# Retention pipelined by head, and band attention with projections and output slabs between its heads

## The chip, the cores and the metric

The kernel runs on one core of one Trainium2 chip. The metric is the device time of one execution in microseconds (us). Engines: TensorE (matrix products), ScalarE (activations, copies), VectorE (elementwise), SyncE (issues the DMAs); GpSimd does next to nothing here.

## What is computed

Two blocks follow each other on 256 tokens of width 1024, all in float32. The first has two layers: layer 0 is a retention mixer and a dense SwiGLU, layer 1 a band attention and a mixture of 8 experts; each ends with a per-layer embedding. The second block (two layers of a hybrid mixer and an MLP) is not touched. What the change touches is this, cut from the reference:

```python
def retention_mixer(xn, positions, w_in, gn_gain, w_o):       # 4 heads, qk 256, v 512
    q, k, v, g = split(xn @ w_in)                             # widths 1024, 1024, 2048, 2048
    q, k = rotary(q), rotary(k) * 256 ** -0.5
    o = chunkwise_retention(q, k, v)                          # decay-weighted (q k^T) v, by head
    o = rmsnorm(o, gn_gain)                                   # over each head's 512
    return (silu(g) * o) @ w_o                                # 2048 -> 1024

def band_attention_mixer(xn, kp, vp, w_q, rel_table, w_o):    # 16 heads of 64
    s = q_c @ k_band^T + bias;  a = softmax(s);  o = a @ v_band
    return o @ w_o
```

At 256 tokens the band covers every earlier chunk.

## The kernel before

Tokens lie in two tiles of 128 (TT = 2), the width in eight chunks of 128 (KD = 8). Each engine runs its own stream of instructions in the order in which its function writes them, and waits on semaphores; nothing reorders them.

**Weights** come as slabs of 1 MB (128 x 2048 float32), in the order that `weight_stream` lists, into a ring of five slots (RING). A projection of 256 columns is one "tall" slab, one of 512 columns two "wide" slabs, and two row chunks of an output matrix one "rows" slab. Every product of two float32 matrices is made of three products of rounded parts (`split_products`, L211: high x high, high x low, low x high), so each slab is split first: ScalarE writes its rounded high part (`scalar_split`, L689) into one of three buffers (HIGHS), and VectorE subtracts it in place to leave the low part (`vector_lows`, L702). Both run two slabs ahead of the one in use (AHEAD), and the high part of slab n waits until slab n-3 has been read. Activations are split in the same way (`vector_norm` L645, `vector_split` L710 and L712) and announced on `parted`. Small products of attention (scores, values, transposes) are plain float32.

**Results** go to PSUM banks: two rings of two banks, `a` (drained by ScalarE) and `v` (drained by VectorE), and four banks that sum an output product.

**Retention** (`tensor_retention` and its namesakes on ScalarE and VectorE): after the norm, eight tall projections of q and k with the rotary on VectorE, four wide ones of v, the scores of the four heads, four wide ones of the gate g. Before the first rotary VectorE makes the table of sines (`vector_constants`). Then, for each head and token tile, values on TensorE (plain float32, 12 products of 512 columns), squares and a root on ScalarE (L997, L583), the gating on VectorE (L1039); after all heads (semaphore `gated`) 32 transposes (L968), gains (L1048) and a split per token tile; then the output product r.out, eight slabs.

**Band attention** (`tensor_band` and its namesakes): four tall projections of k, two wide ones of v, four tall ones of q, then the 16 heads in `tensor_attention` as a software pipeline: in each turn the scores of one head (two products), the three transposes of the probabilities of another (L1207), and the values of a third (two products). VectorE adds the bias and takes the maximum (L1284), ScalarE the exponentials (L1242), VectorE divides (L1300), ScalarE copies the transposed probabilities (L1268) and the head's result (L1275). After all heads VectorE splits the result, and the output product a.out reads its four slabs.

## Time and profile before

| | us |
|---|---|
| median of three runs | 2751.07 (2742.73 to 2752.49) |
| the profiled execution | 2758.43 |
| its span | 2756.60 |
| TensorE busy in the span | 2576.8 (93%) |
| VectorE, ScalarE busy | 1884.1 (68%), 1461.9 (53%) |

TensorE holds 83% of the chain that ended last, VectorE 11%, ScalarE 4%. The page's line of the granted TensorE clock, in 40 slices of 68.9 us, is 9 tenths or more in all slices but the ninth and tenth (6 and 7) and two at 8. The clock has two levels, 2.4 GHz (granted 1.0) and 1.2 GHz (0.5). A busy TensorE is not one that runs at its peak: its records get longer when the clock is lower. Retention lies between about 20 and 240 us of the span, band attention between 486 and 654.

### The profile page before, as it was taken

To read this page: it belongs to the slowest core of one execution; us is meant where nothing else is said; L and a number is where in the kernel's file an instruction comes from. 1 tells how busy PE (TensorE), PEld (TensorE's weight loads), DVE (VectorE), ACT (ScalarE), POOL (GpSimd) and SP (SyncE) were. 2 spreads that over 40 slices of the span, in tenths; PEclk is the share of its full clock that TensorE was granted. 3 is DMA by queue.
4 is the path that set the end of the run, shared out by engine and by line. 5 is a ranking of instruction groups with operands and counts; after the bars stand their busy time and mean duration, and the time that the engine had idled before them with its cause. 6 is when DMAs were issued, how large, how long until landed. Compare 5 with 4: busy or idle time off the path is not lost.

```text
span 2756.6 us, 32701 instructions
## 1 busy us (share of the span) xinstructions
PE 2576.8 (93%) x13559; PEld 2172.2 (79%) x13559; DVE 1884.1 (68%) x1960; ACT 1461.9 (53%) x1347; POOL 0.2 (0%) x4
## 2 busy tenths in 40 slices
PE   7989999896999999999999989799989999998999
PEld 7858897865788888888888777588758988876898
DVE  7454545545788888888888787557675556767554
ACT  3434334443666766767676666455544335555442
POOL 0000000000000000000000000000000000000000
PEclk9999999967999999999999999899989999998999
DMA  7534764415899999989899977255224554522453
GB/s 225 177 107 157 208 191 160 138 61 198 302 352 343 352 342 323 368 327 370 322 370 325 359 262 269 67 157 174 77 92 155 197 170 151 171 86 88 157 187 134
DMA packets 301812, 597.59 MB, mean 217 GB/s; under 512 B 13552, under 2 KB 105952, under 8 KB 301664
## 3 DMA queue, kind: packets, MB, share of 16 engines
q1 hardware_dynamic: 301664, 595.50, 62.7%
q8 instruction: 108, 1.77, 0.3%
q14 instruction: 40, 0.33, 0.0%
HBM read 594.41 MB, written 1.05 MB: 216 GB/s over the span
## 4 chain that ended last, share of the span: by engine, by line
PE 83%; DVE 11%; ACT 4%; issue 2%; DMA 1%; SPq 0%; DVEq 0%; ACTq 0%
PE ps L211 81%; DVE ring_rounded L702 2%; ACT high_rounded L689 1%; DVE arena_rounded L1884 1%; PE ps L1632 1%; PE ps L1207 1%; DMA ring<-in_w_down_dense 1%; DVE arena L2369 0%; DVE h L852 0%; DVE ring_rounded L1884 0%; DVE xT L639 0%; DVE xT_rounded L645 0%; DVE arena L2499 0%; DVE arena_rounded L712 0%; ACT high_rounded L1687 0%
## 5 line engine op out<-in xcount | busy, mean ns | idle before, releaser
L211 PE MATMUL ps<-high_rounded,arena_rounded 128*128 128x512 f32 x2664 | 838.0, 396 | 24.5 <-DVE arena_rounded L712 12.4
L702 DVE TENSOR_TENSOR ring_rounded<-ring,high_rounded 128x2048 fp32r<-128x2048 f32 (+3 forms) x231 | 513.5, 2231 | 328.3 <-ACT high_rounded L689 327.3
L689 ACT ACTIVATE high_rounded<-ring 128x2048 fp32r<-128x2048 f32 (+3 forms) x231 | 430.2, 1864 | 401.0 <-PE ps L211 386.6
L211 PEld LDWEIGHTS ps<-high_rounded,arena_rounded 128*128 128x128 f32 x2664 | 500.9, 191 | 130.5 <-DVE arena_rounded L712 14.3
L211 PE MATMUL ps<-ring_rounded,arena_rounded 128*128 128x512 f32 x1000 | 396.3, 396 | 0.0
L211 PE MATMUL ps<-xT_high_rounded,high_rounded 128*128 128x256 f32 x1280 | 365.8, 286 | 25.2 <-DVE xT_rounded L645 11.2
L211 PE MATMUL ps<-xT_high_rounded,ring_rounded 128*128 128x256 f32 x1280 | 364.0, 284 | 0.0
L211 PE MATMUL ps<-xT_rounded,high_rounded 128*128 128x256 f32 x1280 | 363.8, 284 | 0.0
L211 PE MATMUL ps<-arena_rounded 128*128 128x512 f32 x864 | 339.2, 393 | 0.0
L1884 DVE TENSOR_TENSOR arena_rounded<-arena,high_rounded 128x2048 fp32r<-128x2048 f32 x131 | 297.4, 2288 | 27.4 <-ACT high_rounded L1687 27.2
L1687 ACT ACTIVATE high_rounded<-arena 128x2048 fp32r<-128x2048 f32 x131 | 251.0, 1919 | 84.6 <-PE ps L211 83.2
L211 PEld LDWEIGHTS ps<-xT_high_rounded,high_rounded 128*128 128x128 f32 x1280 | 246.9, 193 | 30.6 <-DVE xT_rounded L645 12.0
L211 PE MATMUL ps<-high_rounded,xT_high_rounded 128*128 128x512 f32 (+2 forms) x640 | 250.5, 391 | 7.7 <-ACT arena L1144 3.1
L211 PEld LDWEIGHTS ps<-xT_rounded,high_rounded 128*128 128x128 f32 x1280 | 249.6, 195 | 0.0
L211 PEld LDWEIGHTS ps<-xT_high_rounded,ring_rounded 128*128 128x128 f32 x1280 | 246.4, 192 | 1.4
L211 PE MATMUL ps<-high_rounded,xT_rounded 128*128 128x512 f32 (+2 forms) x640 | 247.0, 386 | 0.0
L211 PE MATMUL ps<-ring_rounded,xT_high_rounded 128*128 128x512 f32 (+2 forms) x640 | 246.9, 386 | 0.0
L211 PEld LDWEIGHTS ps<-ring_rounded,arena_rounded 128*128 128x128 f32 x1000 | 191.0, 191 | 42.0
L211 PEld LDWEIGHTS ps<-arena_rounded 128*128 128x128 f32 x864 | 162.2, 188 | 35.7
L211 PE MATMUL ps<-arena 128*128 128x128 f32 (+7 forms) x776 | 168.4, 373 | 19.7 <-DVE arena_rounded L1896 5.0
L1884 DVE TENSOR_TENSOR ring_rounded<-ring,high_rounded 128x2048 fp32r<-128x2048 f32 x72 | 162.8, 2287 | 12.7 <-ACT high_rounded L1687 12.4
L211 PE MATMUL ps<-xT_high_rounded,arena_rounded 128*128 128x512 f32 x536 | 169.7, 398 | 1.1 <-DVE arena_rounded L1896 1.1
(282 smaller groups left out, 3084.3 us busy)
## 6 DMA issues: line engine op xcount, KB each, us to landing
arena<-in_w_down_moe SPq DMA_DIRECT2D x76, 1024.0 KB, 5.2
arena<-in_w_up_moe SPq DMA_DIRECT2D x72, 1024.0 KB, 5.8
arena<-in_w_gate_moe SPq DMA_DIRECT2D x68, 1024.0 KB, 5.4
ring<-in_w_in SPq DMA_DIRECT2D x50, 1024.0 KB, 5.1
ring<-in_w_gate_moe SPq DMA_DIRECT2D x44, 1024.0 KB, 5.4
ring<-in_w_up_moe SPq DMA_DIRECT2D x40, 1024.0 KB, 5.7
ring<-in_w_down_moe SPq DMA_DIRECT2D x36, 1024.0 KB, 5.3
ring<-in_w_up SPq DMA_DIRECT2D x32, 1024.0 KB, 5.4
```

The source lines that it names most:

```text
L211: return self.pe.matmul(out, lhsT, rhs, start=start, stop=stop, skip_group_check=True)
L689: act.activation(as_rounded(m, m.highs[n % HIGHS][:, 0:size]), m.slots[n % RING][:, 0:size], ACT.Copy).then_inc(m.rounded, 1)
L702: dve.tensor_tensor(as_rounded(m, slot), slot, as_rounded(m, m.highs[n % HIGHS][:, 0:size]), ALU.subtract).then_inc(m.slabs_split, 1)
L1207: ins = pe.transpose(bank[:, b * P:(b + 1) * P], p[:, b * P:(b + 1) * P], m.ident)
L1632: ins = pe.transpose(bank[:, c * P:(c + 1) * P], m.m_s[:, c * P:(c + 1) * P], m.ident)
L1687: act.activation(as_rounded(m, run.high(k)), run.slot(pos), ACT.Copy).then_inc(m.m_rounded, 1)
L1884: dve.tensor_tensor(as_rounded(m, slot), slot, as_rounded(m, run.high(k)), ALU.subtract).then_inc(m.m_split, 1)
```

## The change

Retention: the v projections now come first, on a first tile that needs only one token tile's parts (`tensor_wide_first`, there before); ScalarE and VectorE split the first two slabs among the parts of the norm (`opening`), and the table of sines stands behind the first v group. Of the four gate groups two come before the scores, one after them, and the last lies inside head 0. Values, norm, gating, transposes and split go head by head, and each head's two r.out slabs are multiplied while the next head is prepared.

Band attention: v's first half, k0 and q0 come first; the heads follow as turns, with one head's scores, the transposes and values of the one before, and one piece of other work between those: a half of a tall projection (`tensor_tall_half`: one bank, 256 columns), a tile of v's second half, or a half of an a.out slab (`tensor_rows_tile`). The splits of slabs that ran ahead of the heads are now inside the turns listed in BAND_SLABS. The pipeline is two heads deep where it was four. `tensor_head_values` and `tensor_head_turned` hold the products and transposes of one head that stood in `tensor_retention`; `vector_head_gated` and `vector_head_turned` the same for VectorE, with means and roots for both tiles at once.

```diff
win = w["w_in_a"][0]
     out = []
+    for h in range(HEADS_R):
+        out += wide("r.v", win, 2048 + h * DV_R)
     for h in range(2 * HEADS_R):
         out += tall("r.qk", win, h * DK_R)
-    for h in range(HEADS_R):
-        out += wide("r.v", win, 2048 + h * DV_R)
     for h in range(HEADS_R):
         out += wide("r.g", win, 4096 + h * DV_R)
     out += rows("r.out", w["w_out_a"][0], 0, 16)
     out += mlp_slabs("dense", (w["w_gate_dense"][0], w["w_up_dense"][0]), w["w_down_dense"][0],
                      FF_DENSE // STEP_FF)
     out += ple_slabs(w, 0)
-    for c in range(4):
-        out += tall("a.k", w["w_kv"], c * 256)
-    for g in range(2):
-        out += wide("a.v", w["w_kv"], D + g * 512)
-    for c in range(4):
-        out += tall("a.q", w["w_q_b"][0], c * 256)
+    keys = [tall("a.k", w["w_kv"], c * 256) for c in range(4)]
+    values = [wide("a.v", w["w_kv"], D + g * 512) for g in range(2)]
+    queries = [tall("a.q", w["w_q_b"][0], c * 256) for c in range(4)]
+    out += values[0] + keys[0] + queries[0] + keys[1] + queries[1] + keys[2] + queries[2]
+    out += values[1] + keys[3] + queries[3]
     out += rows("a.out", w["w_out_b"][0], 0, 8)
...
     for t in range(TT if casts else 0):
+        if opening:
+            scalar_split(act, L, m, 1 if t else -1)
         for half in range(2):
...
+        if opening and t == 0:
+            vector_lows(dve, L, m, 0)
...
+def tensor_tall_half(pe, L, m, w, f, x, ring):
+    if f == 0:
+        pe.wait_ge(m.slabs_split, L.read)
+    pe.wait_ge(ring.drained, L.room(ring))
+    bank = L.bank(ring)
+    for k in range(KD):
+        first, ins = L.split_products(bank[:, 0:S], [p[:, k, f * P:(f + 1) * P] for p in w],
+                                      [p[:, k, :] for p in x], k == 0, k == KD - 1)
+        L.give_back(first)
+    ins.then_inc(ring.full, L.up(ring.full))
+    if f:
+        L.done_with()
+    return L.emptied(ring)
...
+def tensor_rows_tile(pe, L, m, w, t, x, chunk, first, last):
+    n = w[0].shape[1]
+    for c in range(n):
+        for half in range(2):
+            end = last and c == n - 1
+            begin, ins = L.split_products(m.ps[:, 2 * t + half, :],
+                                          [p[:, chunk + c, t * P:(t + 1) * P] for p in x],
+                                          [p[:, c, half * 512:(half + 1) * 512] for p in w],
+                                          first and c == 0, end)
+            L.give_back(begin)
+            if end:
+                ins.then_inc(m.acc_full, L.up(m.acc_full))
+    if t:
+        L.done_with()
...
+def tensor_head_out(pe, L, m, h, half):
+    if half == 0:
+        pe.wait_ge(m.parted, L.next(m.parted))
+    if h == 0 and half == 0:
+        pe.wait_ge(m.acc_drained, L.sums_taken())
+    tensor_rows(pe, L, m, "r.out", parts(m, m.r_yT, m.r_yT_high), 4 * h + 2 * half, h == 0 and half == 0,
+                h == HEADS_R - 1 and half == 1)
 def tensor_retention(pe, L, m):
-    pe.wait_ge(m.parted, L.next(m.parted, 4))
+    x = parts(m, m.xT, m.xT_high)
+    tensor_wide_first(pe, L, m, "r.v", x, m.a)
+    for g in range(3):
+        tensor_wide(pe, L, m, "r.v", x, m.a)
     for h in range(2 * HEADS_R):
-        tensor_tall(pe, L, m, "r.qk", parts(m, m.xT, m.xT_high), m.v)
-    for g in range(4):
-        tensor_wide(pe, L, m, "r.v", parts(m, m.xT, m.xT_high), m.a)
+        tensor_tall(pe, L, m, "r.qk", x, m.v)
+    for g in range(2):
+        tensor_wide(pe, L, m, "r.g", x, m.a)
     for h in range(HEADS_R):
         if h == 0:
...
-    for g in range(4):
-        tensor_wide(pe, L, m, "r.g", parts(m, m.xT, m.xT_high), m.a)
+    tensor_wide(pe, L, m, "r.g", x, m.a)
     pe.wait_ge(m.v.drained, L.emptied(m.v))
     pe.wait_ge(m.a.drained, L.emptied(m.a))
+    tensor_head_values(pe, L, m, 0)
+    w = [L.slab("r.g"), L.slab("r.g")]
+    tensor_wide_tile(pe, L, m, w, 0, x, m.a)
+    tensor_head_turned(pe, L, m, 0)
+    tensor_wide_tile(pe, L, m, w, 1, x, m.a)
     for h in range(HEADS_R):
+        if h + 1 < HEADS_R:
+            tensor_head_values(pe, L, m, h + 1)
+        tensor_head_out(pe, L, m, h, 0)
+        if h + 1 < HEADS_R:
+            tensor_head_turned(pe, L, m, h + 1)
+        tensor_head_out(pe, L, m, h, 1)
...
+    head_sums(0)
+    scalar_split(act, L, m)
+    gate(3, 0)
+    scalar_split(act, L, m)
+    gate(3, 1)
+    for h in range(1, HEADS_R):
+        head_sums(h)
+        scalar_split(act, L, m, 2)
+    scalar_split(act, L, m, 2)
...
+    for g in range(4):
+        vector_lows(dve, L, m, 2)
+        if g == 0:
+            vector_constants(dve, L, m)
+    dve.wait_ge(m.sines, L.next(m.sines, 2))
...
-    dve.wait_ge(m.v.drained, L.at(m.v.drained))
-    dve.memset(m.small[:, 189:190], 0.0).then_inc(m.gated, L.up(m.gated, 8))
-    for t in range(TT):
-        for g in range(4):
-            dve.wait_ge(m.v.full, L.next(m.v.full))
-            bank = L.filled(m.v).rearrange("p (c n) -> p c n", c=4)
-            gain = m.gain[:, G_RET + 4 * g:G_RET + 4 * g + 4].unsqueeze(2).broadcast_to([P, 4, P])
-            dve.tensor_tensor(m.r_yT[:, 4 * g:4 * g + 4, t * P:(t + 1) * P], bank, gain, ALU.mult).then_inc(
-                m.v.drained, L.up(m.v.drained))
-        dve.wait_ge(m.v.drained, L.at(m.v.drained))
-        vector_split(dve, L, m, m.r_yT[:, :, t * P:(t + 1) * P], m.r_yT_high[:, :, t * P:(t + 1) * P])
-    vector_lows(dve, L, m, 8)
+        if h == HEADS_R - 1:
+            L.up(m.a.drained, 2)
+            dve.wait_ge(m.a.drained, L.at(m.a.drained))
+        vector_head_gated(dve, L, m, h)
+        vector_lows(dve, L, m)
+        vector_head_turned(dve, L, m, h)
+        vector_lows(dve, L, m)
+    vector_lows(dve, L, m, 2)
     vector_add_acc(dve, L, m)
...
+def tensor_band(pe, L, m):
+    x, x2 = parts(m, m.xT, m.xT_high), parts(m, m.xT2, m.xT2_high)
+    o = parts(m, m.a_o, m.a_o_high)
+    evicted = {}
+    held = {}
+    rows = lambda h: slice(DH * (h % 2), DH * (h % 2) + DH)
+    def project(name, c, f):
+        if f == 0:
+            held["w"] = L.slab("a.k" if name == "k" else "a.q")
+        evicted[name, c] = tensor_tall_half(pe, L, m, held["w"], f, x if name == "k" else x2, m.a)
+    def values(t):
+        if t == 0:
+            held["v"] = [L.slab("a.v"), L.slab("a.v")]
+        tensor_wide_tile(pe, L, m, held["v"], t, x, m.a)
+        evicted["v", 1] = L.emptied(m.a)
+    def product(c, t):
+        if t == 0:
+            held["o"] = L.slab("a.out")
+            pe.wait_ge(m.slabs_split, L.read)
+            pe.wait_ge(m.parted, L.next(m.parted))
+        tensor_rows_tile(pe, L, m, held["o"], t, o, 2 * c, c == 0, c == 3)
+    tensor_wide_first(pe, L, m, "a.v", x, m.a)
+    evicted["v", 0] = L.emptied(m.a)
+    for f in range(2):
+        project("k", 0, f)
+    pe.wait_ge(m.parted, L.next(m.parted, 4))
+    for f in range(2):
+        project("q", 0, f)
+    for turn in range(HEADS_A + 1):
+        if turn < HEADS_A:
+            if turn % 4 == 0:
+                pe.wait_ge(m.a.drained, max(evicted["k", turn // 4], evicted["q", turn // 4]))
+            tensor_scores(pe, L, m, m.a_q[rows(turn), turn // 2, :], m.a_k[rows(turn), turn // 2, :], m.v)
+        if turn:
+            pe.wait_ge(m.probs, L.next(m.probs))
+            tensor_turn_probs(pe, L, m, m.p_buf[(turn - 1) % 3])
+            turned = L.emptied(m.a)
+        if turn < 2:
+            project("kq"[turn], 1, 0)
+            project("kq"[turn], 1, 1)
+        elif turn < 6:
+            project("kq"[turn // 2 - 1], 2, turn % 2)
+        elif turn < 8:
+            values(turn % 2)
+        elif turn < 12:
+            project("kq"[turn // 2 - 4], 3, turn % 2)
+        elif turn == 12:
+            pe.wait_ge(m.acc_drained, L.sums_taken())
+            product(0, 0)
+            product(0, 1)
+        elif turn < 15:
+            product(1, (turn + 1) % 2)
+        elif turn == 15:
+            product(2, 0)
         h = turn - 1
-        if 0 <= h < heads:
-            vector_head_probs(dve, L, m, h, p[h % 3])
-def tensor_band(pe, L, m):
-    pe.wait_ge(m.parted, L.next(m.parted, 4))
-    for c in range(4):
-        tensor_tall(pe, L, m, "a.k", parts(m, m.xT, m.xT_high), m.a)
-    for g in range(2):
-        tensor_wide(pe, L, m, "a.v", parts(m, m.xT, m.xT_high), m.a)
-    pe.wait_ge(m.parted, L.next(m.parted, 4))
-    for c in range(4):
-        tensor_tall(pe, L, m, "a.q", parts(m, m.xT2, m.xT2_high), m.a)
-    pe.wait_ge(m.a.drained, L.emptied(m.a))
-    rows = lambda h: slice(DH * (h % 2), DH * (h % 2) + DH)
-    tensor_attention(pe, L, m, HEADS_A, lambda h: m.a_q[rows(h), h // 2, :], lambda h: m.a_k[rows(h), h // 2, :],
-                     lambda h, t: m.a_v[:, t, h * DH:(h + 1) * DH], m.p_buf, m.pT_buf)
-    pe.wait_ge(m.parted, L.next(m.parted, 2))
-    tensor_out(pe, L, m, "a.out", parts(m, m.a_o, m.a_o_high), 0, KD)
+        if h >= 0:
+            if h in (0, 8):
+                pe.wait_ge(m.a.drained, max(turned, evicted["v", h // 8]))
+            else:
+                pe.wait_ge(m.a.drained, turned)
+            tensor_values(pe, L, m, h, lambda t: m.a_v[:, t, h * DH:(h + 1) * DH], m.pT_buf[h % 2])
+    product(2, 1)
+    product(3, 0)
+    product(3, 1)
+    evict(m.a_v[:, 0, 0:512])
+    scalar_split(act, L, m)
+    evict(m.a_v[:, 1, 0:512])
+    scalar_split(act, L, m)
+    scalar_split(act, L, m)
+    for f in range(2):
+        evict(m.a_k[:, f, :])
+    scalar_split(act, L, m)
+    for f in range(2):
+        queries(0, f)
+    for turn in range(HEADS_A + 1):
+        h = turn - 1
+        if h >= 0:
+            scalar_turned_probs(act, L, m, m.pT_buf[h % 2])
+        if turn < HEADS_A:
+            scalar_head_exps(act, L, m, turn, m.s_buf[turn % 3], m.p_buf[turn % 3])
+        if turn == 0:
+            evict(m.a_k[:, 2, :])
+            evict(m.a_k[:, 3, :])
+        elif turn == 1:
+            queries(1, 0)
+            queries(1, 1)
+        elif turn in (2, 3):
+            evict(m.a_k[:, 4 + turn % 2, :])
+        elif turn in (4, 5):
+            queries(2, turn % 2)
+        elif turn in (6, 7):
+            evict(m.a_v[:, turn % 2, 512:1024])
+        elif turn in (8, 9):
+            evict(m.a_k[:, 6 + turn % 2, :])
+        elif turn in (10, 11):
+            queries(3, turn % 2)
+        if h >= 0:
+            scalar_head_out(act, L, m, h, m.a_o[:, h // 2, :])
+        if turn in BAND_SLABS:
+            scalar_split(act, L, m)
+    scalar_split(act, L, m)
+BAND_SLABS = (0, 1, 2, 4, 6, 7, 8, 10, 12, 13, 15)
+    def part(c):
+        at = slice(2 * c, 2 * c + 2)
+        dve.wait_ge(m.a.drained, L.at(m.a.drained))
         vector_split(dve, L, m, m.a_o[:, at, :], m.a_o_high[:, at, :])
-    vector_lows(dve, L, m, 4)
+    for turn in range(HEADS_A):
+        vector_head_logits(dve, L, m, turn, m.s_buf[turn % 3],
+                           lambda h, t: m.bias[:, h, TILE_KEYS[t]][:, ::-1], 1.0)
+        vector_head_probs(dve, L, m, turn, m.p_buf[turn % 3])
+        if turn in (5, 9, 13):
+            part(turn // 4 - 1)
+        if turn:
+            L.up(m.a.drained, 2)
+        if turn < 2:
+            L.up(m.a.drained, 2)
+        elif turn < 12:
+            L.up(m.a.drained)
+        if turn in BAND_SLABS:
+            vector_lows(dve, L, m)
+    L.up(m.a.drained, 2)
+    part(3)
+    vector_lows(dve, L, m)
```

How the order on the engines moves, at three places. ScalarE at the opening (`xn<-h` is the norm's sum of squares, `xT_high` the cast of normed parts, `high<-ring` a slab's high part), before:

```order
L601 ACTIVATE xn,small<-h 128x1024
L604 ACTIVATE small<-small 128x1
L614 ACTIVATE xT_high_rounded<-xT 128x4x128 x4
L689 ACTIVATE high_rounded<-ring 128x2048 x2
L913 ACT_TABLE_LOAD
```

and now:

```order
L599 ACTIVATE xn,small<-h 128x1024
L602 ACTIVATE small<-small 128x1
L692 ACTIVATE high_rounded<-ring 128x2048
L615 ACTIVATE xT_high_rounded<-xT 128x4x128 x2
L692 ACTIVATE high_rounded<-ring 128x2048
L615 ACTIVATE xT_high_rounded<-xT 128x4x128 x2
L692 ACTIVATE high_rounded<-ring 128x2048 x2
L1058 ACTIVATE arena<-ps 128x512 x2
L692 ACTIVATE high_rounded<-ring 128x2048 x2
L1058 ACTIVATE arena<-ps 128x512 x2
L950 ACT_TABLE_LOAD
```

One slab is rounded ahead of each token tile's casts, and the sines' table load has moved behind two v groups (L1058 is their copy out of PSUM). VectorE in the tail of retention, before (the last of eight gatings, the barrier, then gains and splits of whole token tiles):

```order
L588 TENSOR_SCALAR small<-small 128x1
L591 RECIPROCAL small<-small 128x1
L1039 SCALAR_TENSOR_TENSOR arena<-ps,small,arena 128x512
L1042 MEMSET small 128x1
L1048 TENSOR_TENSOR arena<-ps,gain 128x4x128 x4
L710 CAST arena_rounded<-arena 128x16x128
L712 TENSOR_TENSOR arena_rounded<-arena,arena_rounded 128x16x128
```

and now, for one head (`ring_rounded<-ring` is a slab's low part):

```order
L586 TENSOR_SCALAR small<-small 128x2
L589 RECIPROCAL small<-small 128x2
L1086 SCALAR_TENSOR_TENSOR arena<-ps,small,arena 128x512 x2
L705 TENSOR_TENSOR ring_rounded<-ring,high_rounded 128x2048
L1096 TENSOR_TENSOR arena<-ps,gain 128x4x128 x2
L713 CAST arena_rounded<-arena 128x1024
L715 TENSOR_TENSOR arena_rounded<-arena,arena_rounded 128x1024
L705 TENSOR_TENSOR ring_rounded<-ring,high_rounded 128x2048
```

The barrier is gone, and two slabs' low parts lie inside each head. ScalarE among the heads of band attention, before (copy of the transposed probabilities, two exponentials of the next head, again a copy, the head's result):

```order
L1268 ACTIVATE arena<-ps 128x384
L1242 ACTIVATE arena,small<-arena,small 128x128
L1242 ACTIVATE arena,small<-arena,small 128x256
L1268 ACTIVATE arena<-ps 128x384
L1275 ACTIVATE arena<-ps 64x256
```

and now, one turn with a slab:

```order
L1318 ACTIVATE arena,small<-arena,small 128x128
L1318 ACTIVATE arena,small<-arena,small 128x256
L1448 ACTIVATE arena<-ps 128x256
L1343 ACTIVATE arena<-ps 64x256
L692 ACTIVATE high_rounded<-ring 128x2048
L1336 ACTIVATE arena<-ps 128x384
```

Between the exponentials and the next copy of probabilities now stand a projection's copy (L1448), the head's result (L1343) and a slab's high part (L692).

## Rows read from the trace of the kernel before

**Rows 1.** Windows: stretch, length, busy TensorE, its loads, VectorE, ScalarE, GpSimd; clock, DMA.

```profile
19.70:26.50 6.80, 3.96 (x18) 3.99 (x19) 6.18 (x8) 3.50 (x3) 0.00 (x0) 0.50 1.08 366
165.40:193.40 28.00, 17.14 (x57) 8.27 (x57) 16.13 (x34) 10.09 (x26) 0.00 (x0) 0.95 0.11 38
190.40:197.30 6.90, 5.56 (x18) 4.75 (x19) 6.06 (x7) 0.00 (x0) 0.00 (x0) 0.51 0.00 0
...
497.10:500.90 3.80, 3.75 (x19) 3.75 (x20) 3.80 (x5) 1.59 (x1) 0.00 (x0) 0.56 0.00 0
...
567.70:626.90 59.20, 56.47 (x176) 31.65 (x176) 22.86 (x128) 28.98 (x96) 0.00 (x0) 0.57 0.05 19
572.70:623.90 51.20, 50.94 (x146) 28.51 (x146) 19.39 (x108) 24.13 (x82) 0.00 (x0) 0.50 0.00 1
...
631.20:654.00 22.80, 22.76 (x94) 18.73 (x95) 5.91 (x5) 4.56 (x6) 0.00 (x0) 0.94 0.42 139
...
1923.00:1960.00 37.00, 35.10 (x212) 29.98 (x211) 33.89 (x45) 17.04 (x15) 0.00 (x0) 1.00 0.34 114
```

**Rows 2.** Timeline of the opening: start, length, instruction, idle time before it.

```profile
13.04 0.63 ACT L614 ACTIVATE xT_high_rounded<-xT 128x512 fp32r<-128x512 f32 x1 [4.36 <-DVE xT L639]
14.63 1.47 DVE L645 TENSOR_TENSOR xT_rounded<-xT,xT_high_rounded 128x512 fp32r<-128x512 f32 x2
22.54 0.55 PE L211 MATMUL ps<-xT_high_rounded,high_rounded 128*128 128x256 f32 x1 [5.62 <-issue]
24.56 0.28 DVE L879 CAST arena<-arena 128x256 f32<-128x256 int32 x1
30.99 0.29 DVE L905 TENSOR_SCALAR arena<-arena 128x256 f32<-128x256 f32 x1
37.44 0.36 PE L211 MATMUL ps<-xT_high_rounded,high_rounded 128*128 128x256 f32 x1 [1.56 <-DVE arena L1014]
```

**Rows 3.** DMAs of slabs issued from 6 to 7 us, their landing.

```profile
L2761 SPq DMA_DIRECT2D ring<-in_w_in_a x3: 434/655/4834, 5.6 to 6.8; - x3
...
DMA to landing us min/median/max: 9.3/11.9/14.2
```

**Rows 4.** Timeline of TensorE in the tail of retention.

```profile
164.37 0.40 PE L211 MATMUL ps<-ring_rounded,xT_high_rounded 128*128 128x512 f32 x1
165.50 2.81 PE L211 MATMUL ps<-arena 128*128 128x512 f32 x6 [0.73 <-issue]
...
184.07 1.09 PE L968 MATMUL ps<-const,arena 128*128 128x128 f32 x8 [2.45 <-DVE small L1042]
...
193.36 1.20 PE L211 MATMUL ps<-high_rounded,arena_rounded 128*128 128x512 f32 x2
```

**Rows 5.** Timeline of band attention, by engine.

```profile
491.84 1.47 DVE L645 TENSOR_TENSOR xT_rounded<-xT,xT_high_rounded 128x512 fp32r<-128x512 f32 x2
...
561.76 1.90 ACT L689 ACTIVATE high_rounded<-ring 128x2048 fp32r<-128x2048 f32 x1
563.70 2.29 DVE L702 TENSOR_TENSOR ring_rounded<-ring,high_rounded 128x2048 fp32r<-128x2048 f32 x1 [3.47 <-ACT high_rounded L689]
569.45 0.92 PE L211 MATMUL ps<-arena 64*128 64x128 f32 x4 [0.84 <-DVE small L1284]
...
624.13 0.55 PE L1207 MATMUL ps<-const,arena 128*128 128x128 f32 x3
624.23 0.38 ACT L1275 ACTIVATE arena<-ps 64x256 f32<-64x256 f32 x1 [0.78 <-PE ps L211]
624.76 0.84 PE L211 MATMUL ps<-arena 128*64 128x256 f32 x4
```

**Rows 6.** Chain that ended last: start, length, engine, line.

```profile
497.15 69.86 PE ps L211 x480
...
568.75 0.29 DVE arena L1284
...
571.45 0.55 PE ps L1207 x3
```

176 lines of the change are left out of this document (71 added, 105 removed).

## The prediction

> **What bounds the kernel now.** I read the page's line of the granted clock first (the section on the profile tells it), to see where TensorE runs slowly, and found the one long dip in the band attention and just behind it. Then the table of windows [rows 1], to see in the stretches that the change touches whether TensorE waits, runs slowly, or neither; then the timelines and the chain there [rows 2 to 6]. Nearly everywhere TensorE is busy and ends the chain, so a change gains only what TensorE waits, or what it runs at 1.2 instead of 2.4 GHz. Both are to be found here. In the tail of retention, 165.4 to 193.4, TensorE is busy 17.14 of 28.00 us. Between 572.7 and 623.9, the heads of band attention, it is busy 50.94 of 51.20 us, but at a granted 0.50, the lower level: that is a loss the busy share hides. ScalarE and VectorE are busy 24.13 and 19.39 us there, so under half [rows 1].
>
> All sums are made against the profiled execution: span 2756.60, run 2758.43 us, so 1.83 us lie around it. That run is 7.4 us above the median 2751.07 of the three runs; I take the gain off the median.
>
> **Opening of retention.** The first product was r.qk and is now r.v with a wide first tile, which needs only the first token tile's parts and one slab at a time. Before, it started at 22.54, after VectorE's subtractions of both tiles and the first slab's low part, and waited another 1.56 us at 37.44, because VectorE made the sine table between two slabs [rows 2]. Now ScalarE rounds slab 0 ahead of its casts. Slab 0 is issued at 5.6 and lands 9.3 us later, at 14.9; the third, issued at 6.8, lands 14.2 later, at 21.0 [rows 3], so one comes every 3 us. So: high part 14.9 + 1.9 (a slab's high part, 561.76 in [rows 5]) = 16.8, cast 0.6 = 17.4, VectorE's two subtractions 1.5 = 18.9 [rows 2], low part 2.3 (563.70 in [rows 5]) = 21.2. TensorE starts 1.2 us earlier. But the clock is at the lower level until 26.5 in the window from 19.7 [rows 1], TensorE having stood idle after its transposes, so of 1.2 us only 0.6 is work done. The sine table now falls under the first r.v groups, whose tiles take 5.7 us each. The first tile, 2.6 us of it done at 26.5, ends at 29.5, the second at 35.2, the second group at 46.5. Slab 0 is read in the middle of the second tile, 32.4, so slab 3's high part ends at 34.3 and its low part at 36.6; the table, 24.6 to 31.3 before [rows 2], adds 6.7, and slab 4's low part 2.3: 45.6, and TensorE wants it at 46.5. The 1.56 us goes, with a cover of 0.9 us only. **Gain 0.6 + 1.6 = 2.2 us.** Bounds: 0.6 if that cover fails, 4.8 if the early start keeps the clock up (2.6 more).
>
> **Tail of retention.** From the end of r.g at 164.8 to the first r.out product at 193.4 are 28.6 us [rows 4]. TensorE's own work in it is 12 value products, three in 2.81, so 11.2 us, 32 transposes at eight in 1.09 to 1.25, some 4.7 us, and 0.7 us in which the last gate is evicted (it stays). 28.6 - 16.6 = 12.0 us are waits for norm chains, the barrier after all heads and VectorE's splits. The clock then sits at 0.51 from 190.4 to 197.3, with TensorE busy 5.56 of it [rows 1]: 2.8 us lost, 0.6 of them in the transposes counted already, 2.2 in the first out products. Now a group r.g and the 16 r.out half-products stand between the heads. Is the cover enough? Head 0, from the start of its values: second product ends 2.8, ScalarE squares it by 3.6, means, table load 1.28, root and reciprocal by 5.5, VectorE gates both tiles by 7.0; TensorE has a gate tile until 2.8 + 5.5 = 8.3. For later heads: values of h+1, then 5.4 us of r.out (two row slabs per head, 24 products each; eight slabs took 46 us with the slow start), then its transposes. Again about 1.3 us spare. The table is loaded twice more and ScalarE evicts the same eight tiles: all under these products. The two slabs per head need 4.2 us of ScalarE and VectorE each, against 15 us per head. **Gain 12.0 + 2.2 = 14.2 us.** Bounds: 9 if each of four heads comes 2.5 us later than reckoned (1.3 covered), 15.
>
> **Start of band attention.** The parts of the first token tile are ready at 493.3 [rows 5]; the first projection started at 497.15 [rows 6] since it waited for all four. The wide first tile starts on two: 3.85 us. The second tile's parts come at 497.1, its products at 498.9. The idle time ahead of 497.15 was followed by a lower clock, 0.56 over 497.1 to 500.9 [rows 1], so 3.3 us at half and 1.7 lost; without that gap I take it as gone. **Gain 5.5 us**, bounds 3.8 and 5.5.
>
> **Heads of band attention.** 16 heads took 59.2 us (567.7 to 626.9) [rows 1]. At the full clock one head's work is 0.92 (scores) + 0.50 (three transposes; the row's 0.55 overlaps its neighbour) + 0.84 (values) [rows 5], 2.26 us, 16 of them 36.2: 23.0 us less. Now the projections k1, q1, k2, q2, v1, k3, q3 and the first five half-slabs of the out product stand between. Does the clock hold? The nearest stretch in the trace is 1923 to 1960, where 2.8 us pieces of a projection alternate with 2 us of small plain-fp32 products and TensorE also waits a little (busy 35.10 of 37.00): granted 1.00 [rows 1]. So yes, in the forecast.
>
> The out product used to wait 4.3 us (626.9 to 631.2) for the split of all heads, and ran its first part slowly: 0.94 over 22.80 us [rows 1] is 1.4 us lost. Now only the last two chunks' split is late, and a 2.7 us half-slab lies over it. 5.7 us.
>
> Against that stands a **new wait**. The slabs' rounding, which had finished before the heads, now lies inside 11 of the turns on ScalarE and VectorE, in order with the softmax. Let V be the end of a head's values on TensorE in a turn with a slab. ScalarE copies the head out (0.38), rounds the slab, VectorE subtracts: from 561.76 to the end of the latter's 563.70 row are 4.2 us [rows 5]. Only then come the next head's maxima on VectorE, the exponentials and the division: 2.70 us from 568.75 to the transposes at 571.45 [rows 6]. With 0.1 us of hand-over the probabilities are ready at V + 7.4. TensorE gets to those transposes after a whole turn and the next scores. A half projection is half of 5.68 us (68.2 us for 12 slabs, the 69.86 of [rows 6] less 1.7), so a turn is 0.92 + 0.50 + 2.84 + 0.84 = 5.1 and it is there at V + 6.0: it waits 1.4 to 1.5. If the turn after has a whole projection (turns 1, 7) it is there at V + 8.7 and waits for nothing. If the turn after has a slab too, the ScalarE and VectorE loop sets the pace, about 7.0 us a turn, and 1.9 are waited. Slabs are in turns 0, 1, 2, 4, 6, 7, 8, 10, 12, 13 (15 has none left to round). The waits: after 1, 4, 7, 12 some 1.5 each, after 2, 8, 13 some 1.8, after 10 about 1.9 (the scores of head 12 wait for the last query's eviction behind the exponentials). Sum 13.3. The wait for the first query's eviction, 0.7, is as before. **Gain 23.0 + 5.7 - 13.3 = 15.4 us.** Bounds for the waits: 0 and 20.
>
> **Sum.** 2.2 + 14.2 + 5.5 + 15.4 = 37.3. Profiled 2758.4 - 37.3 = 2721; median 2751.1 - 37.3 = 2714 us. Behind the band nothing is reordered, and the experts' slabs start no later. The DMA queue fetches the same slabs in another order and holds them longer; among the heads its share was 0.05 [rows 1], so it has room.
>
> **Rivals.** B, *no new waits*: the rounding slips into gaps, the heads are bound by TensorE alone: 13.3 us more, 2701. Against it the in-order queues; for it that each wait is under 2 us, so small errors of mine cancel it.
>
> C, *the waits cost clock*: each of the eight waits comes with a stretch at the lower level as after 19.7 and 190.4, where 6.8 and 6.9 us ran at half [rows 1], 3.4 us a piece: 27 us for all, 2741; for half of them 2727. For it speaks that waits here are followed by such stretches; against it that those waits were 3.5 us and longer, and that 1923 to 1960 held through waits of 0.5 and 1.1.
>
> The Trainium skill's page TensorE: Matmul & The Clock Gate says, under A second HAM failure mode, that short pauses between groups of matmuls that cycle through PSUM banks make the clock swing; that is this rival, and speaks against the change.
>
> D, *slower than before*: the heads' small fp32 products alone hold the clock down, projections or not. The row 572.7 to 623.9 shows that TensorE need not be idle for it. Then everything from the first scores to the last values is at 1.2 GHz: 59 us of projections and out products double, the heads lose their 23 again, the 13.3 of waits are covered: 69 us on top, 2783. It decides from the point where 54% of that stretch is at half (37.3 of 69). The row of 1923 to 1960 speaks against it.
>
> On the same page, under What's actually happening, an idle TensorE is what brings the lower clock and activity what lifts it. This trace disagrees for the heads: 99% busy and 0.50. By the page alone the heads would have had the full clock already, the 23.0 us would not be there to gain, and the time would be 2737; the row decides.
>
> E, *retention's cover is too thin*: 5 to 8 us less, 2720.
>
> **Chances.** Forecast 0.55, B 0.15, C 0.18, D 0.04, E 0.08. The range takes in B with the opening's 2.6 more, 2697, and C for half of the waits together with E, 2736; the three runs before spread over 10 us, which is less. What 0.5% can tell is about the limit of measuring this kernel, 13.8 us. Only D is above 2765; a full C, or C with E, ends between 2737 and 2765. Faster 0.92, same 0.04, slower 0.04.
>
> **What would show it.** Opening: first product about 21.3, no wait of 1 us or more in the first 60 us. Tail: from the last gate tile of the third group to the last r.out product no wait over 1 us, clock 1.00. Band: first product as soon as two parts are there; heads at clock 0.95 or more; waits of 1.4 to 1.9 us on the division of the probabilities in turns 3, 4, 6, 9, 10, 14 and 15, on the scores in turn 12, none in 2 and 8, summing to some 13; no wait over 1 us ahead of the last out products. Wrong would be: a clock near 0.5 among the heads (D), waits absent (B), or waits in retention on the gating of a head (E).

## The result and the profile after

The changed kernel took 2706.03 us (median of 4 runs, 2699.85 to 2708.31) where the kernel before took 2751.78 beside it (4 runs, 2742.73 to 2754.20): ratio 0.9829, 95% interval 0.9808 to 0.9849. The gain is 45.7 us where 37.3 were forecast; 2706 lies inside the range 2697 to 2736. The same kernel was run five more times later: 2711.38 beside 2749.69, ratio 0.9853, interval 0.9834 to 0.9871. So the gain is some 38 to 46 us, and the forecast of 37.3 stands just below it. (Gains in us are differences of medians; a ratio is made of all the runs, so it can differ from theirs in the fourth digit.)

The page of the profiled execution after (span 2698.0 us, the shortest of all its runs), with its busy tenths in 40 slices and the granted clock of TensorE:

```profile
span 2698.0 us, 32714 instructions
PE 2526.2 (94%) x13559; PEld 2136.9 (79%) x13559; DVE 1883.0 (70%) x1959; ACT 1465.1 (54%) x1353; POOL 0.2 (0%) x4
...
PEclk9999999998999999999999999999989999998999
```

In the page of before the ninth and tenth digits of the clock were 6 and 7: the heads of band attention at half the clock, and the router behind them. The heads' part is gone; the 8 that is left there, in the slice from 607 to 674, holds the router's stretch. (Two more digits of 8 stand in both pages, and the page of before has a third.) TensorE runs the same 13559 products in 50.6 us less busy time (2576.8 before), which is most of the 58.6 by which the two spans differ. So most of the difference is the same products at a higher clock, and only the rest is idle time removed. A part of it lies behind the band, in code that the change doesn't touch; the table by stage below takes that out.

Windows of the changed stretches after (columns: stretch, its length, busy time and instructions of each engine, granted clock, share of the DMA engines, GB/s). They answer [rows 1]:

```profile
20.50:148.40 127.90, 127.75 (x752) 112.44 (x752) 80.24 (x81) 53.85 (x41) 0.00 (x0) 0.99 0.58 195
148.40:218.20 69.80, 68.76 (x297) 52.85 (x296) 43.46 (x44) 30.79 (x37) 0.00 (x0) 1.00 0.45 151
467.60:606.20 138.60, 126.67 (x750) 104.17 (x751) 66.90 (x164) 68.15 (x140) 0.00 (x0) 0.98 0.35 114
512.20:515.60 3.40, 3.40 (x17) 3.40 (x18) 1.62 (x1) 2.24 (x2) 0.00 (x0) 0.54 0.00 0
```

The first line is retention up to the third gate group: TensorE is never without work. The second is the pipelined heads with the last gate group and the out product: 1.04 us idle, clock 1.00, where the tail before held 10.86 us of idle time in 28.00 [rows 1, 4]. The third is all of band attention from the first projection: the clock is back at 0.98, but 11.9 us are idle, and 10.8 of them are the new waits that the prediction named. The fourth line is explained below.

Timeline of TensorE after (start, duration, engine, line, operation, tiles, shape, count, and in brackets the idle time ahead and what ended it): the first product of retention, then every place behind the first product of the band where TensorE waited, but for the 0.47 before the first scores. It answers [rows 2, 5]:

```profile
20.53 0.47 PE L211 MATMUL ps<-high_rounded,xT_high_rounded 128*128 128x512 f32 x1 [4.45 <-DVE ring_rounded L705]
...
512.18 0.67 PE L1298 MATMUL ps<-const,arena 128*128 128x128 f32 x3 [1.44 <-DVE arena L1368]
518.89 0.55 PE L1298 MATMUL ps<-const,arena 128*128 128x128 f32 x3 [0.16 <-DVE arena L1368]
530.39 0.55 PE L1298 MATMUL ps<-const,arena 128*128 128x128 f32 x3 [1.45 <-DVE arena L1368]
552.13 0.55 PE L1298 MATMUL ps<-const,arena 128*128 128x128 f32 x3 [1.44 <-DVE arena L1368]
558.84 0.55 PE L1298 MATMUL ps<-const,arena 128*128 128x128 f32 x3 [1.77 <-DVE arena L1368]
571.29 0.92 PE L211 MATMUL ps<-arena 64*128 64x128 f32 x4 [1.79 <-ACT arena L1448]
586.26 0.55 PE L1298 MATMUL ps<-const,arena 128*128 128x128 f32 x3 [1.55 <-DVE arena L1368]
592.43 0.55 PE L1298 MATMUL ps<-const,arena 128*128 128x128 f32 x3 [1.24 <-DVE arena L1368]
597.59 0.86 PE L211 MATMUL ps<-arena 128*64 128x256 f32 x4 [0.58 <-ACT arena L1336]
```

L1298 is the transposes of a head's probabilities, L1368 VectorE's division of them. These are turns 3, 4, 6, 9, 10, 14 and 15, and the scores of head 12: the eight places that the prediction named. The ninth row, 0.58 us before the values of the last head, is one that it did not name. The chain of waits through one of them (start, duration, what), which answers [rows 6]:

```profile
523.53 1.92 ACT high_rounded L692
525.46 0.02 issue
525.48 2.29 DVE ring_rounded L705
527.77 0.20 DVE arena L1352
...
528.36 0.18 DVE small L1357
528.54 0.02 issue
528.57 0.99 ACT arena L1318 x4
529.56 0.02 issue
529.58 0.18 DVE small L1364
529.76 0.02 issue
529.78 0.56 DVE arena L1368 x2
530.35 0.04 issue
530.39 0.55 PE ps L1298 x3
```

ScalarE rounds the slab (L692), VectorE subtracts (L705), and only then come the next head's maxima (L1352), the exponentials (L1318), the division (L1368) and TensorE. From the start of L692 it is 6.86 us to the transposes.

**Stage by stage.** One profile is one run, and the experiments below brought more profiles with the old or the new form of each stage. The table gives each stage from marks that all have: the last addition of retention's out product to the residual, the first product of the band, the start of the last pair of additions of its out product.

| stage | old form | new form | gain | forecast |
|---|---|---|---|---|
| to the last addition of retention | 240.4 (mean of 9, 238.6 to 241.9) | 219.4 (mean of 4, 218.9 to 220.3) | 21.0 | 2.2 + 14.2 |
| from there to the first band product | 254.2 (10, 252.1 to 257.0) | 251.3 (4, 248.8 to 252.7) | 2.9 | 3.85 |
| first band product to last additions | 157.8 (3, 156.9 to 159.6) | 138.7 (3, 138.6 to 138.9) | 19.1 | 17.1 |
| behind the band (the code is the same) | 2096.8 to 2102.6 | 2091.8, 2098.5, 2099.9, 2103.3 | none | 0 |

The forecast of the third row is 15.4 plus the 1.7 us of clock that the prediction counted with the start. The rows sum to 43.0 us, between the 45.7 and the 38.3 of the two comparisons. The profiled executions alone differ by 58.6 us: the profile of before is near the long end of its stretch behind the band (2102.6), the first one of after is the shortest of all (2091.8), on the same instructions. That is 10.8 us which the change did not make.

### The profile page after: what moved, and what is told of

It is laid out like the page before. It is cut to its first block, busy times and chain, and to the rows that moved or that the text cites. A ratio compares the mean times of both kernels' runs of the same rounds, so it can differ in the third digit from the quotient of the medians.

```text
span 2698.0 us, 32714 instructions
## 1 busy us (share of the span) xinstructions
PE 2526.2 (94%) x13559; PEld 2136.9 (79%) x13559; DVE 1883.0 (70%) x1959; ACT 1465.1 (54%) x1353; POOL 0.2 (0%) x4
## 4 chain that ended last, share of the span: by engine, by line
PE 81%; DVE 11%; ACT 4%; issue 2%; DMA 1%; SPq 0%; DVEq 0%; ACTq 0%
PE ps L211 80%; DVE ring_rounded L705 3%; ACT high_rounded L692 2%; DVE arena_rounded L2040 1%; PE ps L1788 1%; DMA ring<-in_w_down_dense 1%; DVE arena L2525 0%; DVE h L890 0%; DVE arena L2655 0%; DVE ring_rounded L2040 0%; ACT arena L1318 0%; DVE xT_rounded L646 0%; DVE xT L640 0%; DMA ring<-in_w_in_a 0%; PE ps L1298 0%
## 5 line engine op out<-in xcount | busy, mean ns | idle before, releaser
L705 DVE TENSOR_TENSOR ring_rounded<-ring,high_rounded 128x2048 fp32r<-128x2048 f32 (+3 forms) x231 | 513.2, 2230 | 289.9 <-ACT high_rounded L692 288.9
L692 ACT ACTIVATE high_rounded<-ring 128x2048 fp32r<-128x2048 f32 (+3 forms) x231 | 430.4, 1864 | 365.3 <-PE ps L211 339.0
L211 PEld LDWEIGHTS ps<-high_rounded,arena_rounded 128*128 128x128 f32 x2664 | 494.5, 188 | 125.2 <-DVE arena_rounded L715 9.0
L211 PE MATMUL ps<-xT_high_rounded,high_rounded 128*128 128x256 f32 x1280 | 362.2, 283 | 14.7 <-DVE xT_rounded L646 8.4
L211 PE MATMUL ps<-xT_rounded,arena_rounded 128*128 128x512 f32 x528 | 166.7, 397 | 0.0
```

Source lines behind the costliest of these rows:

```text
L211: return self.pe.matmul(out, lhsT, rhs, start=start, stop=stop, skip_group_check=True)
L692: act.activation(as_rounded(m, m.highs[n % HIGHS][:, 0:size]), m.slots[n % RING][:, 0:size], ACT.Copy).then_inc(m.rounded, 1)
L705: dve.tensor_tensor(as_rounded(m, slot), slot, as_rounded(m, m.highs[n % HIGHS][:, 0:size]), ALU.subtract).then_inc(m.slabs_split, 1)
```

## The experiments

All of them are compared with the kernel before, run on the same chip.

**1. Each half alone.** Are the two halves independent, and what is each worth? The first kernel has the change's retention and the old band (and the old order of its slabs), the second the old retention and the change's band:

```
first kernel:   retention (slab order, opening, tensor, scalar, vector) of the change; band of before
second kernel:  band (slab order, tensor, scalar, vector) of the change; retention of before
```

> The change's retention (opening and head pipeline) with the band attention of before. Theory T (the parts are independent and add up as the two traces show: opening 5.0, tail 16.3, norm behind it 1.6, together 22.9 of the 45.0 of the changed stages): about 2729 us, ratio 0.9917, the band's stretch as before (some 157 us from its first product to its last out product, TensorE at the lower clock among the heads). By the prediction's own terms, 2.2 + 14.2 = 16.4, it would be 2735. Rival R (part of the gain is only the profiled run's luck with the clock behind the band): the gain of this half and that of the band alone would sum to clearly less than 45.

Measured: 2730.27 us (5 runs) beside 2753.28, ratio 0.9918, interval 0.9904 to 0.9933.

> The change's band attention with the retention of before. Theory T: start 3.8 and inner part 18.3, 22.1 together: about 2730 us, ratio 0.9920, new waits on the division of the probabilities in the same turns as in the change (3, 6, 9, 10, 14, 15) and on the scores in turn 12. By the prediction's terms, 5.5 + 15.4 = 20.9, 2731. Rival R: the band gains 45 less what retention alone gains only if nothing outside them moves; a sum of the two halves under 40 speaks for R.

Measured: 2729.98 us (5 runs) beside 2753.28, ratio 0.9919, interval 0.9901 to 0.9936. The halves gain 23.0 and 23.3 us, 46.3 together. The whole change gained 45.7 and 38.3 in its two comparisons. Each half's interval reaches some 4 to 5 us to either side, and within that the halves add up: rival R, a sum clearly under 45, does not show, and theory T holds for both. The start of the band shows in TensorE's timeline, in the first kernel (old form) and the second (new form):

```profile
473.73 0.39 PE L211 MATMUL ps<-xT_high_rounded,high_rounded 128*128 128x256 f32 x1 [4.01 <-DVE xT_rounded L647]
```

```profile
493.27 0.50 PE L211 MATMUL ps<-high_rounded,xT_high_rounded 128*128 128x512 f32 x1 [0.23 <-DVE xT_rounded L647]
```

The wait of 4.01 us for all four parts becomes 0.23 us for the first two. The first kernel's heads still run at the lower clock while TensorE works, seen in the window over them:

```profile
547.00:615.40 68.40, 63.35 (x179) 36.57 (x180) 26.39 (x120) 28.19 (x89) 0.00 (x0) 0.50 0.02 6
```

**2. The opening alone.** The values' projections ahead of the queries' and keys', slab 0 rounded ahead of the casts, the constants behind the first group. Two of the four gate groups stand ahead of the scores here, where before all four came behind them; the rest is as before:

```diff
-    pe.wait_ge(m.parted, L.next(m.parted, 4))
...
-    for g in range(4):
-        tensor_wide(pe, L, m, "r.v", parts(m, m.xT, m.xT_high), m.a)
+    x = parts(m, m.xT, m.xT_high)
+    tensor_wide_first(pe, L, m, "r.v", x, m.a)
+    for g in range(3):
+        tensor_wide(pe, L, m, "r.v", x, m.a)
```

> Only the opening: r.v before r.qk, slab 0 rounded ahead of the casts, first tile on one token tile's parts, constants behind the first r.v group; the gates keep two groups ahead of the scores and the other two behind; tail and band as before. Theory T: 5.0 us, of it 2.0 the earlier first product, 1.6 the wait for the second slab's low part that goes, the rest a lower clock for 3.4 instead of 6.8 us: 2747, ratio 0.9982; by the prediction 2.2 us, 2749.5. In the profile: first product near 20.5, no wait over 1 us before 60 us, the lower clock for 3.4 us. Rival: the short lower-clock stretch was one run's luck; then 6.8 us at half as before and 3.3 us of gain.

Measured: 2749.93 us (12 runs) beside 2753.28, ratio 0.9991, interval 0.9982 to 1.0000. The ratio makes it 2.5 us, with 0 to 5; the medians differ by 3.4. TensorE's first product and the window at the lower clock:

```profile
20.66 0.77 PE L211 MATMUL ps<-high_rounded,xT_high_rounded 128*128 128x512 f32 x1 [3.90 <-DVE ring_rounded L707]
```

```profile
19.00:25.80 6.80, 5.14 (x12) 4.11 (x13) 6.21 (x6) 2.75 (x4) 0.00 (x0) 0.50 1.05 395
```

The start and the wait came as expected; the short stretch at the lower clock did not. Of five profiles with this opening three have 3.4 us of it and two 6.8. The nine profiles with the old opening all have 6.8. So the short stretch is neither certain, as theory T had it, nor one run's luck, as the rival had it; why it comes in some runs only is open. I had read 5.0 us of gain from the first profile after, 1.7 of them from this stretch, and the prediction's 2.2 was nearer to what the runs show than that reading. The last addition of retention started at 236.7 us, 3.7 before the old form's mean.

**3. The new waits taken away.** The subtraction of a slab moves from the end of a turn into the next one, between that head's maxima and its division:

```diff
     for turn in range(HEADS_A):
         vector_head_logits(dve, L, m, turn, ...)
+        if turn - 1 in BAND_SLABS:
+            vector_lows(dve, L, m)
         vector_head_probs(dve, L, m, turn, ...)
         ...
-        if turn in BAND_SLABS:
-            vector_lows(dve, L, m)
```

> The whole change, with one edit: the subtraction that makes a slab's low part, which VectorE did at the end of a turn and so ahead of the next head's maxima, now stands in the next turn between that head's maxima and its division, while ScalarE makes the exponentials. Theory T (the new waits of 1.2 to 1.8 us come from that subtraction in VectorE's order): VectorE's 1.9 us are gone from the loop, the waits on the division drop from some 9 us to under 2, and the lower-clock stretches that followed them at 512 and 560 go too: about 2695 us, ratio to before 0.979. Rival S (ScalarE's rounding of the slab, which stands ahead of the exponentials, sets the loop): the subtraction now ends after the exponentials, the division is as late as before, and the time stays at 2706, ratio 0.983.

Measured: 2695.66 us (5 runs, 2691.13 to 2700.77) beside 2753.28, ratio 0.9792, interval 0.9775 to 0.9809. Theory T, and the fastest kernel of this study. Waits of TensorE from 480 to 600 us (what waited, for whom, total, times, longest), then the window over the band:

```profile
PE ps L211 <- ACT arena L1336: 0.6, 1, 0.6
PE ps L211 <- ACT arena L1448: 0.5, 1, 0.5
```

```profile
470.80:594.80 124.00, 122.90 (x750) 101.21 (x751) 66.96 (x163) 68.45 (x140) 0.00 (x0) 1.00 0.39 128
```

The same 750 products as in the change's window take 124.0 instead of 138.6 us, with 1.1 us idle. No wait on L1368 is left, and the clock is 1.00. VectorE's order in it shows why:

```profile
523.92 0.29 DVE L1352 CUSTOM_DVE_ANT_0 arena<-ps,arena 128x128 f32<-128x128 f32 x1 [2.33 <-PE ps L211]
...
525.42 2.29 DVE L705 TENSOR_TENSOR ring_rounded<-ring,high_rounded 128x2048 fp32r<-128x2048 f32 x1 [0.65 <-ACT high_rounded L692]
525.80 0.39 ACT L1318 ACTIVATE arena<-arena,small 128x128 f32<-128x128 f32 x1
```

The maxima are done before the slab's high part is, and the 2.29 us of subtraction lie beside the exponentials instead of ahead of them. The rival, that ScalarE's rounding alone would keep the loop as long, falls.

**4. What holds the clock down among the heads?** Before, they ran at 0.50 with TensorE 99% busy [rows 1]. The change puts rounded projections between them, and also removes waits. To part the two, the kernel before got nothing but products whose results are thrown away, behind the transposes of each head, in a bank that is free:

```diff
             tensor_turn_probs(pe, L, m, p[h % 3])
+            for i in range(N):
+                L.mm(m.ps[...one bank...], stationary, moving)
```

> The kernel before, with eight added products (rounded operands, 128 x 128 by 256 columns, into a bank that is free, results thrown away) behind the transposes of each of the 16 heads of band attention; nothing else differs. They take 0.95 us at the full clock. Theory F (what held the clock down was that TensorE had nothing but the small plain-float32 products and transposes; large rounded products between them lift it, and no gap needs to be closed): the heads take 16 x 3.2 = 51 us at a clock of 0.95 or more instead of 59, and the time falls by some 8 us, to 2743, with more work done. Rival G (the clock was low by chance of that stretch or for a reason that the projections don't touch): 16 x (3.88 + 1.9) = 92 us at 0.50, 33 us more, 2784.

> As the run with eight added products per head, with 24: 2.8 us at the full clock, the size of the half projection that the change puts there. Theory F: clock 0.95 or more, heads 16 x 5.1 = 81.6 us, 22 more than before: 2773. Rival G: 16 x (3.88 + 5.7) = 153 us at 0.50, 94 more: 2845. If eight keep the clock low and 24 lift it, the share of the rounded products decides.

> The kernel before, with four added products per head on plain float32 operands (128 x 128 by 256 columns, of the residual, results thrown away), some 1.8 us at the full clock: larger than the heads' own products but of their type. Theory F1 (the type decides: plain float32 doesn't lift the clock): clock 0.50, 16 x (3.88 + 3.6) = 120 us, 60 more: 2811. Theory F2 (the size and the full rows of the array decide): clock 0.95 or more, 16 x (2.26 + 1.8) = 65 us, 6 more: 2757.

Measured: eight rounded products 2748.94 us (10 runs) beside 2751.78, ratio 0.9989, interval 0.9979 to 0.9999; 24 of them 2775.73, ratio 1.0087 (1.0069 to 1.0105); four plain ones 2760.05, ratio 1.0030 (1.0020 to 1.0039). 128 more products made the kernel no slower, if anything 3 us faster. The clock comes up in all three, so the type of the operands is not it (F1 falls). In the run with eight it took longer than I had expected, 13.7 us against 6.8 in the two others. At half the clock that costs 6.8 us, about the 6 by which the run missed the 2743 of theory F. Windows over it, and then from there on:

```profile
567.00:580.70 13.70, 13.70 (x53) 10.40 (x52) 3.86 (x22) 4.83 (x17) 0.00 (x0) 0.54 0.07 27
580.70:620.00 39.30, 38.49 (x241) 28.52 (x239) 16.42 (x91) 20.87 (x70) 0.00 (x0) 1.00 0.00 1
```

Then the forms of the heads' own products, repeated:

> The kernel before with four added products per head of the form of the heads' own value products: plain float32, 128 rows into 64 columns of the array, 256 columns moved, of the residual, results thrown away; 1.7 us per head at the full clock. Theory W (what holds the clock down is that the heads use only half of the array's rows or columns; the added products with all 128 by 128 lifted it): clock stays at 0.50, 16 x (3.7 + 3.4) = 114 us, some 54 more: 2806. Rival X (any longer piece of products between the short ones lifts it): clock 0.95, the heads as long as with the 128 by 128 products of the same length, 2758.

> The same with eight added products per head of the form of the scores: plain float32, 64 rows into 128 columns of the array, 128 columns moved, results thrown away; some 1.85 us per head at the full clock. Theory W: clock stays at 0.50, 16 x (3.7 + 3.7) = 118 us, some 59 more: 2811. Rival X: clock 0.95, 2760. If one of the two lifts the clock and the other not, it is rows or columns of the array that count, not both.

Measured: value form (128 rows into 64 columns) 2751.57 us (10 runs) beside 2749.69, ratio 1.0004 (0.9993 to 1.0014); score form (64 rows, 128 columns moved) 2813.14, ratio 1.0223 (1.0202 to 1.0243). The first lifts the clock though half of the array's columns are unused, the second leaves it low. (The value form took 1.78 us in one head and 0.92 in the next, in turn, where I had expected 1.7 in all: less added work than planned, and the clock came up all the same. No run shows why.) Theory W is wrong as I had put it (rows or columns); what is left is rows, or the length of a product. The last pair holds one and changes the other:

> The kernel before with four added products per head, plain float32, 64 rows into 128 columns of the array, 256 columns moved (results thrown away), some 1.8 us at the full clock. The two runs before differ in two things: the products that lifted the clock used all 128 rows and moved 256 columns, those that left it low used 64 rows and moved 128. Theory N (the rows count): clock 0.50, 16 x (3.7 + 3.6) = 117 us, 58 more: 2808. Theory M (the length of a product counts): clock 0.95 or more, 2755 to 2760.

> The counterpart: eight added products per head, plain float32, all 128 rows into 128 columns, 128 columns moved, some 1.85 us at the full clock, results thrown away. Theory N: clock 0.95 or more, 2755 to 2760. Theory M: clock 0.50, 2811.

Measured: 64 rows with 256 columns moved: 2812.07, 2809.65 and 2806.17 us in three runs, and 2752.70 in the fourth, beside 2752.46. All 128 rows with 128 columns moved: 2760.45 us (6 runs), ratio 1.0034 (1.0018 to 1.0050). Theory N: the rows count, not the length. The cleanest pair is the score form and the last run: eight products, 128 columns of the array, 128 columns moved in both, and only the rows differ, 64 against 128: 2813.14 against 2760.45 us, each beside a kernel before within 3 us of the other. The run with 64 rows and 256 columns moved agrees with it in three of its four runs. Windows 572 to 624 of the four runs, in the order value form, score form, 64 rows long, and 128 rows short:

```profile
572.00:624.00 52.00, 51.12 (x276) 31.79 (x274) 18.93 (x105) 25.38 (x83) 0.00 (x0) 1.00 0.00 1
```

```profile
572.00:624.00 52.00, 52.00 (x192) 39.01 (x191) 9.98 (x56) 12.14 (x41) 0.00 (x0) 0.50 0.00 0
```

```profile
572.00:624.00 52.00, 52.00 (x135) 32.27 (x133) 9.99 (x56) 12.13 (x41) 0.00 (x0) 0.50 0.00 0
```

```profile
572.00:624.00 52.00, 52.00 (x343) 41.77 (x343) 18.31 (x104) 21.80 (x74) 0.00 (x0) 0.95 0.00 1
```

TensorE is busy all the time in the second and third, without one wait, and stays at half. The fourth run of the third kernel is some 55 us shorter, at a mean granted clock of 0.974 (0.952 to 0.955 in the others). It was not profiled; the two numbers fit the full clock among the heads. So these half-row products left the clock low in three of four runs, not in all: they did not bring it up where it had fallen, but it seems that they can also run without its falling. What decides that is open.

**5. The changed kernel once more**, for a second profile:

> The changed kernel as it is, for a second profile and more runs beside the kernel before. Theory L (the first profile of it was a lucky one behind the band, 2091.8 us where the other eight profiles of this study have 2097 to 2103, and in the opening, 3.4 us at the lower clock instead of 6.8): median about 2706 to 2708 us, ratio 0.983, the profile's stretch behind the band 2097 or more, the band from first product to last addition 138 to 139 us with the waits in the same turns. Rival: the change does shorten what follows the band by some 8 us; then 2092 again.

Measured: 2711.38 us (5 runs, 2707.01 to 2716.18) beside 2749.69, ratio 0.9853 (0.9834 to 0.9871). The band is as in the first profile, the stretch behind it is 2098.5 us, not 2091.8: theory L there. The median is 3 us longer than the upper end of what I had expected. Its opening again had 3.4 us at the lower clock, so that part of L did not show here. Its window over the band:

```profile
472.90:611.60 138.70, 126.74 (x750) 104.01 (x751) 66.94 (x164) 68.06 (x139) 0.00 (x0) 0.98 0.35 114
```

## Why the prediction was right, and where it was off

- **Opening, 2.2 forecast.** Alone it gave 2.5 us by the ratio (0 to 5), 3.4 by the medians, and 3.7 in the marks of its one profile. The first product came at 20.53 instead of the reckoned 21.2 (slab 0 landed 8.8 instead of 9.3 us after its issue), and the 1.56 us wait went. The cover of 0.9 us held in all five profiles: no wait there is over 0.12 us.
- **Tail, 14.2 forecast.** The two profiles of before and after give 16.3 us. The mechanism was right: no wait over 1 us is left (68.76 busy of 69.80), no head's gating is late, so rival E fell. The term that was mis-sized is TensorE's own work of 16.6 us. What stands after between the third gate group and the end of the out product is 69.8 us, less 11.4 of the fourth gate group (its two tiles at 5.7), less 43.9 of the out product at the full clock (46.1 before, with 2.2 lost): 14.5, so 2.1 less than I had reckoned. I had summed rows whose durations reach into their neighbours'. From start to next start, eight transposes take 0.79 us after, where I counted 1.09 to 1.25, and three value products 2.2, where I counted 2.81. That makes 4.0 us less. Of it 1.3 is given back, because the group of products behind each head's values takes 5.9 us instead of 5.6; I can't place the remaining 0.6. By the marks of all profiles the tail is worth 21.0 less 3.7, 17.3 us; in four of the ten profiles with the old tail the lower clock in and behind it lasted 10.2 us, not the 6.8 of the one that I had. That can make up the last microsecond, but no run holds it apart.
- **Start of the band, 3.85 + 1.7 forecast.** The wait of 4.01 us became 0.23. From the first transposes of the norm to the first product it is 10.3 us in the old form and 6.4 to 6.5 in the new, 3.8 to 4.0 less, as said. The marks of the table differ by 2.9 only, because they take in the whole stretch between retention and the band, which scatters by 4 to 5 us from profile to profile in either form. All old starts in the profiles have a stretch at the lower clock behind the gap, none of the new ones.
- **Heads of the band, 15.4 forecast.** With the 1.7 of clock 17.1, measured 19.1. The clock came back as said, and rival D fell. A head's own work was mis-sized at 2.26 us: the three transposes take 0.30 us from start to next start where I counted 0.50, 3.2 us in sixteen heads. Without the waits my terms make the band 156.9 - 17.1 - 13.3 = 126.5 us, and experiment 3 measured 124.0: the 3.2 less the 0.58 of the wait before the last values that I had not named. The waits took back 1.4 of that, as follows, and the old form's three profiles are on average 0.9 us longer than the one that I had.
- **The new waits, 13.3 forecast.** They came in the eight places named, 10.8 us in sum, and but for the 0.58 in none where none was said. The largest miss is turn 4: 0.16 instead of 1.8 us. It was paid in another way. After the wait of 1.44 in turn 3 the clock is at 0.54 for 3.4 us (the fourth line of the windows after), TensorE does 1.7 us less work in it and so comes to turn 4's transposes 1.7 us later. With it the sum is 12.5. A second stretch of 3.4 us, from 560.25, costs another 1.7, which makes 14.2, and experiment 3, without waits and stretches, is 14.7 us shorter (138.7 against 124.0). So the term of 13.3 is right to 1.4 us, with the idle part of it smaller and a part in clock that I had not counted.
- **Rival C, waits that cost clock,** was true in small. Two of the eight waits were followed by a stretch at the lower level in both profiles of the change, and three in the profile of the band alone (experiment 1). Which ones differs: the wait in turn 3 each time, the one in turn 10 twice, those in turns 12 and 14 once each. Each stretch is 3.4 us long and so costs 1.7, half of the price that I had taken from stretches of 6.8. When the waits went in experiment 3, so did the stretches. The eight at 3.4 us of loss each of my full case did not come. The Trainium skill's page TensorE: Matmul & The Clock Gate, under A second HAM failure mode, has the rule of short pauses that make the clock swing; the traces agree for two or three waits in eight.
- **Rival B, no new waits, 2701,** is what experiment 3 made of the change by moving one line: 2696.

What I could not know from the trace of before is the other half of D: the heads' products run on at the lower clock without any idle time, once it has fallen, and by experiment 4 D might have come true had the pieces between them been products over half of the rows; no run has the change with such pieces. The row of 1923 to 1960, on which I had decided against D, has full-row projections in it, and by the same experiment that is what mattered. I had read it as a likeness of two stretches and gave no reason why it should carry over, so that step was right with some luck. The same page of the Trainium skill, under What's actually happening, lets activity lift the clock and speaks of how busy TensorE has been. With the busy share of the profile for it, that doesn't fit here: TensorE is busy 52.00 of 52.00 us at 0.50 in two of the runs above.

## What to carry to other kernels

Read the granted clock beside the busy share: a stretch that is 99% busy at 0.50 is worth half its length, and here that was the largest single term of the change. Work that is spread between the heads must be placed in each engine's own order too: a 2.3 us subtraction ahead of the next head's maxima cost 14.7 us of the band's 138.7, and no measurable wait when it stood behind them, where VectorE waits for ScalarE anyway. And sum durations by the distance from start to next start, not by those of the rows, when short products follow each other.

## What the runs showed of the hardware

- The lower clock among the heads began beside the short waits of the first two heads: 0.84 and 1.09 us before 569.45 and 571.45 in the profile of before, lower level from 572.7. All ten profiles with the old heads have it, from 1.9 to 5.0 us behind the first scores. How long it stays then depended on the form of the added products: 6.8 to 13.7 us with any form that uses 128 rows, be it rounded or plain, 64 or 128 columns wide, 128 or 256 columns long; 126.3 us, to the end of the heads and past it, in the profiles of the two forms of 64 rows (one unprofiled run of the second did not lose the clock, by its time). The head's own mixture, scores of 64 rows with transposes and values of 128, stayed low for 51 to 68 us.
- Adding work can be free: 128 more products in the heads, 1.13 us a head at the full clock by their starts, and a ratio of 0.9989.
- The same instructions behind the band took from 2091.8 to 2103.3 us in the profiles, 0.5% of the time. Two profiles that differ by that much outside the changed stages say nothing of the change; the medians and the marks by stage do.
